# Index keys first, index products spread over four jobs, and attention taken two groups at a time with GpSimd scaling the probabilities

## The chip, the cores and the metric

The kernel runs on one core of one Trainium2 chip. The metric is device time in microseconds (us), the median of a few executions. The engines are named as the profile names them: PE is TensorE's matrix products (PEld its weight loads), DVE is VectorE, ACT is ScalarE, POOL is GpSimd, and SP is the queue that loads the weights.

## What is computed

One batch element of 512 tokens, 1024 wide, passes through three blocks in fp32: a gated block with a convolution and an mLSTM, then a block with sparse attention (A), then one with banded window attention (B), each with cross attention to 256 memory rows and a feed-forward stage. The change touches only how A and B attend. In A an indexer of 16 heads of 64 chooses which keys a query may see:

```python
dots = jnp.einsum('bqhd,bsd->bqhs', q_idx, k_idx)          # 16 heads of 64
score = jnp.einsum('bqhs,bqh->bqs', jax.nn.relu(dots), w_idx)
score = jnp.where(causal, score, -inf)
_, idx = lax.top_k(score, 128)                             # TOPK of 512 keys
s = (q_lat @ c_sel + q_rope @ kr_sel) * 128 ** -0.5        # 8 heads
o_lat = jax.nn.softmax(s) @ c_sel
```

B has 16 query heads of 64 over 4 key heads; a query sees the 128 keys up to itself, and one learned logit per head (a sink) joins the softmax's maximum and sum. The cross attention has 4 heads of 64 over 256 keys, with no mask.

## The kernel before, in words

All activations are held transposed, as 8 tiles of 128 features by 512 tokens. A dense product is done in **jobs**: 256 output columns of a weight matrix, 2 x 8 x 3 = 48 products of 128x128x512, three for each pair because operands are split into an upper and a lower fp32r half (L900). For each job SP loads the weights into one of two slots (the job's number decides which), ACT writes the upper half (L1581), POOL subtracts it for the lower half (`lower_job`, L2783), PE multiplies into a pair of banks, and DVE or ACT empties them. The order of the jobs is the table `STAGES`: in A four jobs `a_idx` (index queries, two tiles each), then `a_keys` (index key, rope part of the keys, index weights), `a_kv`, `a_qmem`, four `a_q`, `a_uk`, `a_uv`, and then attention and the output jobs `a_out`. Every engine has its own program, written out by hand; semaphores join them.

**The indexer.** The index queries and the index key are rotated before use. ACT copies the raw rows out, sends them by DMA to their partner rows (`partner_rows`), and DVE multiplies and adds (`turned`, L2567 and L2569), which counts in `rope_ready`. All of tiles 9 to 16 and the key tile 17 were rotated before the first index product. `dots` (L1418) then takes, for the query blocks b = 1, 2, 3 in turn and eight tiles each, two products of 64 rows (two heads), which are the 24 pairs of dots. ACT applies relu in the bank (L2068), and DVE multiplies by the head's weight and adds into `chosen` (L2710). Four pairs are put between the products of `a_kv` and 20 between those of `a_qmem` (at `DOTS_AFTER`). Blocks b = 1 end first here. When a block's sixteen heads are in, DVE runs 16 rounds of the eight largest (L2741) and their replacement (L2743), for b = 1, 2 and 3: 48 rounds of width 256, 384 and 512, with the rotation of the attention's queries (`turn_queries`) put between them at `ROPES_AT`. After the last round comes the mask (L2745), and behind it in DVE's program stands the first step of attention.

**Attention** (`attend`) runs over groups, one head or pair of heads by one block of 128 queries: 32 groups in A with keys 128, 256, 384 and 512 wide, 32 in B (two heads of 128 keys at b = 0, and of 256 at b = 1 to 3), and 8 for the memory behind each. 80 groups in all; a *unit* is four groups, b = 0 to 3. For a group, PE makes the scores (L1313: 128-row products in A, two side by side of 64 rows in B and memory), DVE adds the mask, scales and finds the row's extreme (L2612), ACT takes the exponential and its sum (L2003), DVE inverts the sum (L2628) and scales the probabilities (L2635), PE transposes them (L1322), ACT copies them out of the bank (L2012), and PE multiplies with the values (L1335; 64 columns each in B and memory). Per unit ACT copies the output (L2017) and DVE subtracts for its lower half (L2643). In B DVE first copies the sink into the columns beside the scores (L2607) and takes the lesser of extreme and sink (`lowest`, L2622). PE's program at step g is: scores of g, transposes of g - 3 (`LAG`), sums of g - 5 (`SUM_LAG`). Four of the products of the output job are put between the last steps (`FILL_AT`).

## Time and profile before

| | us |
|---|---|
| median of 3 runs | 2098.12 |
| lowest and highest | 2096.47, 2103.21 |
| the profiled execution | 2096.36 |
| its span, first to last instruction | 2094.6 |
| PE busy in the span | 2059.3 |

A product is counted busy until its modelled end, and each overlaps the next, so a busy PE may still be slower than it could be; what PE costs is read from the distance between the starts of products. The profile's waits show when an engine stood still and which instruction of which engine released it. The granted clock of PE is given as a share of 2.4 GHz.

### The profile page before, as it was taken

How to read it: one execution, taken by the hardware profiler on the slowest of the kernel's cores; microseconds unless marked ns; L12 is line 12 of the kernel's file. 1: busy time of each engine (PE TensorE's matmuls, PEld its weight loads, DVE VectorE, ACT ScalarE, POOL GpSimd, SP SyncE). 2: the span in 40 equal slices, each digit the busy share in tenths (PEclk: the TensorE clock that was granted, in tenths of full speed). 3: DMA queues.
4: the chain of work that ended last, by engine and by line, in shares of the span. 5: the costliest groups of instructions: out<-in, count | busy, mean ns of one | idle time of the engine just before them, and what ended most of it. 6: DMA issues, size and time to landing. Idle time of an engine off the chain costs nothing.

```text
span 2094.6 us, 28597 instructions
## 1 busy us (share of the span) xinstructions
PE 2059.3 (98%) x10618; PEld 1733.8 (83%) x10618; DVE 986.8 (47%) x1909; ACT 886.8 (42%) x1307; POOL 844.6 (40%) x281
## 2 busy tenths in 40 slices
PE   9999999999999999998999999999999999999998
PEld 6888877888888888884878888888887688888887
DVE  4889688573411111366985344134323934431432
ACT  3355445363443222534366454233423954432332
POOL 3443432444244444442712444444443034444443
PEclk9999999999999999999999999999999999999999
DMA  9654312325233342341202432433422034324322
GB/s 370 243 184 125 101 61 61 94 93 181 72 104 86 104 116 78 111 117 43 79 13 57 120 100 86 115 101 95 145 86 73 2 96 119 101 79 122 100 73 88
DMA packets 303799, 219.63 MB, mean 105 GB/s; under 512 B 13568, under 2 KB 288128, under 8 KB 301408
## 3 DMA queue, kind: packets, MB, share of 16 engines
q1 hardware_dynamic: 293216, 195.67, 31.1%
q10 hardware_dynamic: 10496, 22.81, 3.5%
q8 instruction: 53, 0.87, 0.2%
q14 instruction: 34, 0.28, 0.0%
HBM read 213.48 MB, written 2.10 MB: 103 GB/s over the span
## 4 chain that ended last, share of the span: by engine, by line
PE 64%; issue 18%; DVE 10%; POOL 5%; ACT 3%; ACTq 0%; POOLq 0%; DMA 0%; DVEq 0%
PE bank L900 51%; POOL w_split L2783 5%; PE bank L1123 2%; PE bank L1313 2%; PE bank L1335 2%; DVE bank L2280 2%; DVE arena L2743 1%; DVE small L2741 1%; DVE bank L2243 1%; PE bank L1322 1%; PE bank L1171 1%; DVE bank L2222 1%; POOL w_split_out L2783 1%; PE bank L1418 1%; PE bank L1271 1%
## 5 line engine op out<-in xcount | busy, mean ns | idle before, releaser
L900 PE MATMUL bank<-h_hi,w_split 128*128 128x512 f32 x3696 | 1119.3, 381 | 0.7 <-POOL w_split L2783 0.7
L2783 POOL TENSOR_TENSOR w_split<-wslots,w_split 128x2048 fp32r<-128x2048 f32 (+3 forms) x174 | 712.7, 4096 | 971.1 <-ACT w_split L1581 530.5
L900 PEld LDWEIGHTS bank<-h_hi,w_split 128*128 128x128 f32 x3696 | 698.0, 189 | 116.6 <-issue 17.5
L900 PE MATMUL bank<-h_lo,w_split 128*128 128x512 f32 x1848 | 701.3, 379 | 0.0
L900 PEld LDWEIGHTS bank<-h_lo,w_split 128*128 128x128 f32 x1848 | 349.3, 189 | 52.7 <-issue 5.2
L900 PE MATMUL bank<-hid_hi,w_split 128*128 128x512 f32 x1056 | 315.8, 379 | 1.9 <-DVE hid_lo L2525 1.9
L1602 ACT ACTIVATE w_split<-wslots 128x2048 fp32r<-128x2048 f32 (+2 forms) x80 | 141.3, 1767 | 367.9 <-PE bank L900 367.9
L1581 ACT ACTIVATE w_split<-wslots 128x2048 fp32r<-128x2048 f32 (+3 forms) x91 | 158.7, 1744 | 312.8 <-PE bank L900 287.1
L900 PEld LDWEIGHTS bank<-hid_hi,w_split 128*128 128x128 f32 x1056 | 199.6, 189 | 31.5 <-DVE hid_lo L2525 3.2
L900 PE MATMUL bank<-hid_lo,w_split 128*128 128x512 f32 x528 | 200.1, 379 | 0.0
L2243 DVE SCALAR_TENSOR_TENSOR bank<-arena,cols,bank 128x512 f32<-128x512 f32 x240 | 161.4, 749 | 5.5 <-ACT bank L1695 4.9
L2523 DVE TENSOR_TENSOR bank<-arena,bank 128x512 f32<-128x512 f32 x66 | 45.9, 696 | 210.6 <-ACT arena L1915 210.6
L2783 POOL TENSOR_TENSOR w_split_out<-wslots,w_split_out 128x320 fp32r<-128x320 f32 (+1 forms) x28 | 48.8, 1760 | 188.0 <-ACT w_split_out L1581 188.0
L900 PEld LDWEIGHTS bank<-hid_lo,w_split 128*128 128x128 f32 x528 | 99.8, 189 | 14.0
L2670 DVE TENSOR_TENSOR bank<-bank,rstd 128x512 f32<-128x512 f32 x44 | 30.8, 699 | 139.7 <-PE bank L900 139.3
L2482 DVE TENSOR_TENSOR xT<-xT,bank 128x512 f32 (+1 forms) x24 | 16.5, 688 | 139.8 <-PE bank L900 139.8
L2003 ACT ACTIVATE arena<-arena,small 128x257 f32<-128x257 f32 (+5 forms) x128 | 64.2, 503 | 30.3 <-DVE small L2612 16.9
L2525 DVE TENSOR_TENSOR hid_lo<-bank,hid_hi 128x512 f32 x66 | 45.6, 691 | 57.1 <-ACT hid_hi L1917 57.1
L1917 ACT ACTIVATE hid_hi<-bank 128x512 f32 (+1 forms) x66 | 39.4, 598 | 55.5 <-DVE bank L2523 55.5
L1313 PE MATMUL bank<-arena 64*128 64x256 f32 (+5 forms) x256 | 56.3, 425 | 6.2 <-DVE small L2612 4.7
L2675 DVE SCALAR_TENSOR_TENSOR arena<-bank,cols,arena 128x511 f32<-128x511 f32 x44 | 33.0, 750 | 58.1 <-ACT arena L1911 58.1
L563 DVE TENSOR_TENSOR bank<-bank,xT 128x512 f32<-128x512 f32 x24 | 16.9, 706 | 84.7 <-PE bank L900 84.7
(342 smaller groups left out, 2353.3 us busy)
## 6 DMA issues: line engine op xcount, KB each, us to landing
wslots<-in_f_w_up SPq DMA_DIRECT2D x88, 512.0 KB, 4.8
wslots<-in_w_in SPq DMA_DIRECT2D x24, 1024.0 KB, 5.4
wslots<-in_w_ffn_up SPq DMA_DIRECT2D x44, 512.0 KB, 4.6
arena<-in_w_ada ACTq DMA_DIRECT2D x8, 2048.0 KB, 8.9
wslots<-in_f_w_down SPq DMA_DIRECT2D x16, 768.0 KB, 4.8
wslots<-in_a_w_in SPq DMA_DIRECT2D x10, 1024.0 KB, 5.2
wslots<-in_f_w_down SPq DMA_DIRECT2D x16, 640.0 KB, 4.5
arena<-in_w_ada_first SPq DMA_DIRECT2D x8, 1024.0 KB, 18.9
```

What stands on the lines that cost most here:

```text
L900: return nc.tensor.matmul(bank[:], w, woven(x), start=start, stop=stop)
L1123: last = nc.tensor.matmul(banks[2 * p + b // 2][:, (b % 2) * 2 * P:(b % 2 + 1) * 2 * P], h_split[hp][:, c, b * P:(b + 1) * P], woven(w[wp] ...
L1313: last = nc.tensor.matmul(score_bank(g0 + g, e)[:, 0:n], q, kk, start=True, stop=True)
L1335: last = nc.tensor.matmul(unit_bank(unit)[lo:lo + n, b * P:(b + 1) * P], v, probs_turned[:, (g0 + g) % 3, at:at + P], start=(i == 0), stop ...
L1581: nc.scalar.activation(split_of(JOB_STAGE[n], p)[:, 0, 0:size], slot(p, 1, size)[:, 0, :], ACT.Copy).then_inc(hi_ready[p], 1)
L1602: nc.scalar.activation(split_of(name, p)[:, 0, 0:size], slot(p, 1, size)[:, 0, :], ACT.Copy).then_inc(hi_ready[p], 1)
L2003: last = nc.scalar.activation(part, part, ACT.Exp, bias=stat(n, 2 * with_sink + e), scale=-1.0, accum_out=stat(n, 4 + e))
L2243: ins = nc.vector.scalar_tensor_tensor(out=acc, in0=a_pad[:, c, k:k + T], scalar=dw_w[:, c, k:k + 1], in1=acc, op0=ALU.mult, op1=ALU.add)
L2280: ins = nc.vector.scalar_tensor_tensor(out=acc, in0=woven(qk[:, t, k:k + T]), scalar=qk_w[:, t, k:k + 1], in1=acc, op0=ALU.mult, op1=ALU.add)
L2523: nc.vector.tensor_tensor(halves(banks[2 * p][:]), halves(up_gate[:, p, :]), plain(banks[2 * p + 1][:]), ALU.mult).then_inc(S["hid_made"], 1)
L2525: nc.vector.tensor_tensor(hid[1][:, 0:tiles, :][:, t, :], banks[2 * p][:], hid[0][:, 0:tiles, :][:, t, :].bitcast(F32), ALU.subtract).then ...
L2783: last = nc.gpsimd.tensor_tensor(part[:, 1, cols_of], slot(p, 1, size)[:, 0, cols_of], part[:, 0, cols_of].bitcast(F32), ALU.subtract)
```

## The change

**Order of jobs.** `a_keys` comes before the four `a_idx`, so the key tile is rotated first. Each index query tile is rotated after its job, and its dots follow. The 24 pairs go, two tiles at a time and over b = 1, 2, 3, five between the products of each of `a_idx` 2 and 3, eight in `a_kv` (the last six in twos) and six in `a_qmem` (in twos, at products 6, 14 and 22). The first 12 pairs have only banks 5 and 6, so each waits until DVE has used the pair before it. In DVE's program relu's results are weighted (`weighted`) between the rotations. The norm of the latent (`latent_norm`) and the emptying of `a_qmem` move into the rounds of b = 1. PE waits for the former before `a_q`. The rotations of the attention's queries move to later rounds.

**Attention.** PE takes two groups at a step: scores of 2i and 2i + 1, transposes of 2i - 3 and 2i - 2, sums of 2i - 5 and 2i - 4. POOL scales the probabilities in place of DVE, in a new `attend` of its own, with the four pieces of the output job's lower half between groups 30 to 33. ACT copies the transposes of even groups, DVE those of odd ones. In B the sink is given to L2612 as the starting value of its minimum, so `lowest` goes. The eight copies of the key's rope rows, done by POOL before, are one DMA from ACT's queue.

```diff
-    ... ("a_idx", 4), ("a_keys", 1), ("a_kv", 1), ("a_qmem", 1), ...
+    ... ("a_keys", 1), ("a_idx", 4), ("a_kv", 1), ("a_qmem", 1), ...
-        ROPES_AT = {(2, 2): (0, 2), (3, 0): (2, 4), (3, 3): (4, 6), (3, 7): (6, 8)}
+        ROPES_AT = {(2, 8): (0, 2), (3, 2): (2, 4), (3, 9): (4, 6), (3, 13): (6, 8)}
+        DOTS = [(t, b) for j in range(3) for b in range(1, TB) for t in (2 * j, 2 * j + 1)] + [(t, b) for b in range(1, TB) for t in (6, 7)]
+        DOTS_AT = {("a_idx", 2): [(i, k, k + 1) for k, i in enumerate((10, 18, 27, 38, 46))],
+                   ("a_idx", 3): [(i, k + 5, k + 6) for k, i in enumerate((10, 18, 27, 38, 46))],
+                   ("a_kv", 0): [(8, 10, 11), (17, 11, 12), (30, 12, 14), (38, 14, 16), (46, 16, 18)],
+                   ("a_qmem", 0): [(6, 18, 20), (14, 20, 22), (22, 22, 24)]}
+        LATE_DOTS = 12
+        dot_bank = lambda n: banks[(5, 6)[n % 2] if n < 2 * LATE_DOTS else (4, 7, 5, 6)[n % 4]]
...
# PE, attend
-                for g in range(len(groups) + SUM_LAG):
-                    if g < len(groups):
-                        scores(g)
...
-                    if LAG <= g < len(groups) + LAG:
-                        turn(g - LAG)
-                    if g >= SUM_LAG:
-                        sums(g - SUM_LAG)
+                steps = len(groups) // 2
+                for i in range(steps + 3):
+                    of_groups(scores, 2 * i)
...
+                    of_groups(turn, 2 * i - 3)
...
+                    of_groups(sums, 2 * i - 5)
# PE, the dots
+            def dots(first, end):
+                for k in range(first, end):
+                    t, b = DOTS[k]
+                    pe.wait_ge(S["rope_ready"], 10 if k >= LATE_DOTS else 2 + t + 1)
+                    for e in range(2):
+                        before = dot_before(2 * k + e)
+                        if before is not None:
+                            pe.wait_ge(S["relu_used"], before + 1)
...
+            pe.wait_ge(S["norm_ready"], TILES_BEFORE["kv"] + 2)
             for j in range(4):
                 split_job(start_split("a_q", j), DT, 2 * P, h_parts, None)
# DVE, attend
-                def weights(g):
-                    n = g0 + g
-                    steps.settle()
-                    for e, (lo, w) in enumerate(groups[g]["heads"]):
-                        part = probs[:, n % RING, lo:lo + w]
-                        last = nc.vector.tensor_scalar(part, part, stat(n, e), None, ALU.mult)
-                    last.then_inc(S["at_probs"], 1)
+                def copies(g):
...
+                    nc.vector.tensor_copy(probs_turned[:, n % 3, 0:w], banks[6 + n % 2][:, 0:w]).then_inc(S["odd_copied"], 1)
...
+                    if g % 2 and 5 <= g < len(groups) + 4:
+                        copies(g - 4)
# POOL
+            def attend(k, output):
+                g0, groups = GROUPS_BEFORE[k], ATTENTION[k] + ATTENTION[k + 1]
+                for g, grp in enumerate(groups):
+                    n = g0 + g
+                    pool.wait_ge(S["at_inverse"], n + 1)
+                    for e, (lo, w) in enumerate(grp["heads"]):
+                        part = probs[:, n % RING, lo:lo + w]
+                        last = nc.gpsimd.tensor_scalar(part, part, stat(n, e), None, ALU.mult)
+                    last.then_inc(S["at_probs"], 1)
+                    if 30 <= g < 34:
+                        lower_piece(output, ahead(output), g - 30)
```

PE in the middle of B's attention. L1313 (L1323 in the changed kernel) are scores, L1322 (L1332) transposes and L1335 (L1345) sums; before, one unit and the next group stand so in a row:

```order
L1313 MATMUL bank<-arena 128x256 x2
L1322 MATMUL bank<-cons,arena 128x128 x4
L1335 MATMUL bank<-arena 64x128 x4
L1313 MATMUL bank<-arena 128x256 x2
L1322 MATMUL bank<-cons,arena 128x128 x4
L1335 MATMUL bank<-arena 64x128 x4
```

and now, for two steps of two groups:

```order
L1323 MATMUL bank<-arena 128x256 x4
L1332 MATMUL bank<-cons,arena 128x128 x6
L1345 MATMUL bank<-arena 64x128 x8
L1323 MATMUL bank<-arena 128x128 x2
L1323 MATMUL bank<-arena 128x256 x2
L1332 MATMUL bank<-cons,arena 128x128 x8
L1345 MATMUL bank<-arena 64x128 x6
```

The same products stand in half as many runs of one kind. POOL, at the place between the last rotation of A's queries and the first piece of `a_out`'s weights, before:

```order
L2927 TENSOR_TENSOR arena<-arena 32x512 x2
L2949 COPY arena<-arena 32x512 x8
L2783 TENSOR_TENSOR w_split_out_63<-wslots,w_split_out_63 128x320 x4
L2783 TENSOR_TENSOR w_split_out_64<-wslots,w_split_out_64 128x320 x4
```

and now, the first five of 48 scalings (32 groups of one head, 8 of two) behind the rotation:

```order
L2965 TENSOR_TENSOR arena<-arena 32x512 x2
L3003 ISA
L3003 TENSOR_SCALAR arena<-arena,small 128x128
L3003 TENSOR_SCALAR arena<-arena,small 128x256
L3003 TENSOR_SCALAR arena<-arena,small 128x384
L3003 TENSOR_SCALAR arena<-arena,small 128x512
```

The copies are gone from POOL and the scalings have come. PE in `a_qmem`, where L900 (L910) are the job's own products and L1418 (L1431) pairs of dots, before, at b = 2 (the pattern of the 20 pairs):

```order
L1418 MATMUL bank<-arena 128x384 x2
L900 MATMUL bank<-h_lo,w_split_52 128x512
L900 MATMUL bank<-h_hi,w_split_52 128x512
L1418 MATMUL bank<-arena 128x384 x2
L900 MATMUL bank<-h_hi,w_split_52 128x512
L900 MATMUL bank<-h_lo,w_split_52 128x512
L1418 MATMUL bank<-arena 128x384 x2
```

and now, for the two pairs of tiles 6 and 7 at b = 2, with the products before and behind them:

```order
L1431 MATMUL bank<-arena 128x256 x4
L910 MATMUL bank<-h_lo,w_split_52 128x512
L910 MATMUL bank<-h_hi,w_split_52 128x512 x2
L910 MATMUL bank<-h_lo,w_split_52 128x512
L910 MATMUL bank<-h_hi,w_split_52 128x512 x2
L910 MATMUL bank<-h_lo,w_split_52 128x512
L910 MATMUL bank<-h_hi,w_split_52 128x512
L1431 MATMUL bank<-arena 128x384 x4
```

The 24 pairs stand at 18 places instead of 24, and the last of them behind the 22nd product of `a_qmem` instead of the 44th. DVE, around the first round of the eight largest (L2741, `MAX`; L2776 in the changed kernel), before. L2710 (L2626) is the weighting, L2722 (L2655) the latent's norm, L2560 (L2570) the emptying of `a_qmem`:

```order
365 L2710 SCALAR_TENSOR_TENSOR arena<-bank,small,arena 128x512 x3
366 L2722 SCALAR_TENSOR_TENSOR arena<-arena,cols,bank 128x512 x2
367 L2710 SCALAR_TENSOR_TENSOR arena<-bank,small,arena 128x512 x12
368 L2560 TENSOR_TENSOR arena<-bank,rstd 128x512 x2
369 L2725 TENSOR_SCALAR bank<-trig,cons 32x512
370 L2741 MAX small<-arena 128x8
371 L2743 MATCH_REPLACE arena<-small,arena 128x256
```

and now:

```order
374 L2626 SCALAR_TENSOR_TENSOR arena<-bank,small,arena 128x512 x4
375 L2649 RECIPROCAL square<-square 128x128
376 L2776 MAX small<-arena 128x8
377 L2778 MATCH_REPLACE arena<-small,arena 128x256
...
384 L2655 SCALAR_TENSOR_TENSOR arena<-arena,cols,bank 128x512 x2
385 L2776 MAX small<-arena 128x8
...
391 L2570 TENSOR_TENSOR arena<-bank,rstd 128x512 x2
392 L2660 TENSOR_SCALAR bank<-trig,cons 32x512
393 L2776 MAX small<-arena 128x8
```

The norm and the emptying went from ahead of the first round to behind the fourth and the seventh.

## Rows read from the trace of the kernel before

**Rows 1.** The page's part 1: engine, busy us, share of the span, instructions.

```profile
PE 2059.3 (98%) x10618; PEld 1733.8 (83%) x10618; DVE 986.8 (47%) x1909; ACT 886.8 (42%) x1307; POOL 844.6 (40%) x281
```

**Rows 2.** PE's waits, whole run: who for whom, total us, times, longest.

```profile
PE bank L1313 <- DVE small L2612: 4.7, 1, 4.7
PE bank L1418 <- DVE arena L2710: 3.3, 3, 1.8
...
PE bank L1418 <- DVE arena L2569: 2.2, 1, 2.2
PE bank L1322 <- ACT arena L2012: 2.0, 4, 0.7
```

**Rows 3.** PE's timeline, A's attention starts: start, duration, instruction, [idle before].

```profile
1058.37 0.82 PE L1313 MATMUL bank<-arena 128*128 128x128 f32 x4
1063.85 3.36 PE L1313 MATMUL bank<-arena 128*128 128x384 f32 x4 [4.66 <-DVE small L2612]
```

**Rows 4.** Windows: length; PE, PEld, DVE, ACT, POOL busy; clock, DMA, GB/s.

```profile
1061.40:1068.10 6.70, 4.25 (x10) 2.38 (x10) 4.87 (x19) 1.82 (x7) 0.00 (x0) 0.50 0.00 0
1629.54:1636.18 6.64, 6.64 (x60) 4.12 (x58) 6.30 (x40) 6.25 (x22) 0.00 (x0) 1.00 0.00 1
```

**Rows 5.** Timeline of DVE, from the last weighting to the last round.

```profile
995.84 1.29 DVE L2560 TENSOR_TENSOR arena<-bank,rstd 128x512 f32<-128x512 f32 x2
...
997.89 0.43 DVE L2741 MAX8 small<-arena 128x8 f32<-128x256 f32 x1
...
1063.03 0.43 DVE L2745 TENSOR_SCALAR arena<-arena 128x512 f32<-128x512 f32 x1
```

**Rows 6.** Timeline of PE in `a_qmem`: a pair of dots between products.

```profile
968.36 0.70 PE L900 MATMUL bank<-h_hi,w_split 128*128 128x512 f32 x2
968.99 0.92 PE L1418 MATMUL bank<-arena 64*128 64x384 f32 x4
969.84 0.48 PE L900 MATMUL bank<-h_lo,w_split 128*128 128x512 f32 x1
```

**Rows 7.** Waits of DVE from 899 to 998 us.

```profile
DVE bank L2567 <- DMA arena<-arena: 13.8, 4, 5.6
```

**Rows 8.** Timeline of PE in B's attention, one group.

```profile
1632.78 0.70 PE L1313 MATMUL bank<-arena 64*128 64x256 f32 x4
1633.41 0.66 PE L1322 MATMUL bank<-cons,arena 128*128 128x128 f32 x4
1633.99 0.66 PE L1335 MATMUL bank<-arena 128*64 128x128 f32 x8
```

**Rows 9.** Timeline of PE near its end: two groups' sums together.

```profile
1685.23 1.15 PE L1335 MATMUL bank<-arena 128*64 128x128 f32 x16
1686.30 0.48 PE L900 MATMUL bank<-b_out_hi,w_split_out 128*128 128x512 f32 x1
```

**Rows 10.** Timeline of PE in A's attention, where all tiles are whole.

```profile
1086.80 0.60 PE L1322 MATMUL bank<-cons,arena 128*128 128x128 f32 x4
1087.24 0.61 PE L1335 MATMUL bank<-arena 128*128 128x128 f32 x4
```

**Rows 11.** Timeline of POOL, 990 to 1060 us.

```profile
995.89 0.46 POOL L2907 TENSOR_TENSOR arena<-arena,cons 128x128 f32<-128x128 f32 x1 [14.27 <-DVE arena L2710]
...
1002.53 2.52 POOL L2913 TENSOR_TENSOR kv_lo<-arena,kv_hi 128x512 fp32r<-128x512 f32 x2
...
1053.15 4.49 POOL L2949 COPY arena<-arena 32x512 f32<-32x512 f32 x8
```

**Rows 12.** Lines by form, 1622.9 to 1671 us: count, busy us, mean ns.

```profile
L2635 DVE TENSOR_SCALAR arena<-arena,small 128x256 f32<-128x256 f32 x44 | 14.9, 381 | 0.1
...
L2012 ACT ACTIVATE arena<-bank 128x512 f32<-128x512 f32 x21 | 12.1, 575 | 0.0
```

**Rows 13.** Timeline of DVE as POOL begins a piece at 1662.42.

```profile
1661.36 0.16 DVE L2622 TENSOR_TENSOR small<-small,cols 128x2 f32<-128x2 f32 x1
...
1663.44 0.68 DVE L2622 TENSOR_TENSOR small<-small,cols 128x2 f32<-128x2 f32 x1
```

364 lines of the change are left out of this document (191 added, 173 removed).

## The prediction

> **What bounds the kernel now.** I read the page's first part, then the waits of PE, then PE's timeline where the change acts. PE is busy for 2059.3 of 2094.6 us [rows 1] with 10618 products, a count the change doesn't touch. So time can come only from three things: waits of PE; what is lost when the shape of its tiles changes; and its clock. The waits near the change are few: 4.66 us at the start of A's attention for L2612, which stands in DVE's program behind the last round, 3.3 and 2.2 of dots, and 2.0 of transposes at four places [rows 2, 3]. The clock: from 1061.4 to 1068.1 PE's granted clock reads 0.50, the lower level of 1.2 GHz, which came after PE had stood still for 2 us [rows 4], and the first products behind the wait are slow: four, mostly of 384 columns, take 3.36 us [rows 3].
>
> The third thing is hidden in "busy". The reader is to see it in a group of B [rows 8]: scores, transposes and sums start 0.63 and 0.58 us apart, and the sums take another 0.60 to the next group's scores. In A, where every tile is 128x128, four transposes take 1087.24 - 1086.80 = 0.44 [rows 10], so the same four cost 0.14 more in B, between scores of 64 rows and sums of 64 columns. Sixteen sums in a row start 1.07 before what follows [rows 9], and twice eight take 2 x 0.60: 0.12 lost by the break. Two scores of 256 columns on half the rows each are four products; at the rate of transposes (0.11 per 128 columns, halves side by side), they stream in 4 x 0.107 = 0.43, and they take 0.63: 0.20 lost. So one group of B or memory loses about 0.46 to changes of shape, and one of A none.
>
> **Fewer changes of shape.** Two groups at a step halve the number of changes: each pair saves at most 0.20 + 0.14 + 0.12 = 0.46. There are 16 pairs in B and 4 + 4 of memory, so 24 x 0.46 = 11. If the 0.20 in the scores belonged to the products and not to the change, it is 24 x 0.26 = 6.2. A's 16 pairs give nothing, since their tiles are all whole. I take all 0.46, by the same argument that gave the other two numbers, and then see whether the others keep up, since PE's unit of four groups would fall from 6.64 to about 6.64 - 2 x 0.46 = 5.7.
>
> **The other engines at that pace.** In one unit of B, DVE is busy 6.30 and ACT 6.25 of 6.64 [rows 4]; they are as full as PE. DVE loses seven scalings at 0.28 to 0.38 (44 of 256 columns take 0.381 each [rows 12]), 2.5, and `lowest` at 0.16 twice or so, 0.3 to 0.5 [rows 13]; it gains two copies of four and of fewer tiles, as ACT now has them, 0.575 [rows 12], 1.15. DVE stands at 4.7 to 5.0. ACT loses those copies, 6.25 - 1.1 = 5.15. Both are below 5.7. POOL gets seven scalings. No row shows its price: POOL copies 32x512 at 4.49 / 8 = 0.56 each with one input, and multiplies two inputs in 0.46 for 128 columns and 2.52 / 2 = 1.26 for 512 [rows 11], which is 0.73 at 256. The scaling has one tensor as input, so the copy is nearest: a start of about 0.2 (0.46 less 128 columns of the slope) and 0.36 / 2 for half its width, 0.4; I take 0.45, and keep 0.28 (half the copy, with no start) and 0.73 as ends. Then 7 x 0.45 = 3.2 of 5.7: POOL has room for pace.
>
> Latency is tighter. A step lasts 2.8, and the transposes of group 2i - 2 follow its scores by one step and a half, about 3.9 us from the scores' start. In between come the scores 0.70 [rows 8], L2612 at 0.42 twice, the exponential at 0.5 twice and its sums at 0.2 twice, and the inverse at 0.16 (all in the same timelines), and POOL's two scalings 0.9, with some hand-overs: 3.6 to 4.3. Some steps will wait a little. Before, the distance was three groups, 5.5 us. I take three quarters of the 11 us: **8.3**. Ends: 2 (every step waits 0.4) and 11.
>
> DVE and POOL disturb each other: as POOL began a piece, the L2622 beside it took 0.68 instead of 0.16 [rows 13]. Those of two inputs are gone from DVE's attention after the change but for one in four groups (the lower half of the output), so I price this at nothing; 14 scalings longer by 0.3 would still be below PE's pace.
>
> The Trainium skill has a rule against this change: GPSIMD Engine Reference, 3.1, holds that elementwise work goes to DVE, with a two-input add of 2048 taking twice as long on GpSimd. By its factor on DVE's 0.38 a scaling is an estimated 0.76, which is the upper end of my bound, and no row has a one-input multiply on POOL to judge it; the sum above goes by the copy's row. The time by it is the first rival's. The same skill, SBUF — State Buffer, Who interferes with whom, says that DVE with two SBUF inputs locks against GpSimd's reads; by that rule, the trace agrees (0.68 against 0.16).
>
> **Start of A's attention.** DVE's rounds run from 997.89 to 1063.46, 65.6 us, without rest [rows 5]; PE has begun the first four scores at 1058.37, and waits from 1059.19 to 1063.85 [rows 3]. The first round had to wait for the last of `dots`, behind product 44 of 48 of `a_qmem` and begun at 992.43 in PE's timeline, whose weighting ends at 995.84, and for the emptying of that job and a table, 2.05 more [rows 5]. Now the last dots stand behind product 22. Removed from ahead: 22 products at 0.216, 4.8; and those 2.05 and the latent's norm (two instructions, 1.3) now lie inside the rounds, 3.3. Added ahead: the dots of tiles 0 to 5 no longer wait for all the rotations, but each pair of the first 12 waits for DVE, as only two banks serve it. DVE had 13.8 us of waits for the partner rows' DMA [rows 7] in this stretch and has work to fill them now; PE has a gap of 8 to 10 products (about 2 us) between pairs, and a pair's relu and weighting take some 1.6: tight but enough. The key tile first and each index tile behind its own job leave the DMA (5.6 at most [rows 7]) one job of 10.5 us. I let PE be 0 to 5 late in all on these, and take 1 more of waits than before (3.3 + 2.2).
>
> So the last weighting ends at about 995.8 - 4.8 - 2.5 (below) + 1 = 989.5, the rounds start about 990 and last 65.6 + 3.3 = 68.9: 1058.9 instead of 1063.46. PE's arrival: the 24 pairs were at 24 places, and are at 18. A place costs two changes: four products of 384 columns stream in 2 x 0.32 and take 969.84 - 968.99 = 0.85, 0.21 lost, and two products before it take 0.63 instead of 0.43 [rows 6], 0.20. Six fewer: 6 x 0.41 = 2.5 earlier. New waits of PE behind the dots: `a_q` waits for the norm, which DVE reaches four rounds (3.7 us) after the first: about 990 + 3.7 + 1.5 = 995.2, against PE's end of `a_qmem` at about 994.8 - 2.5 + 1 = 993.3. I take 2. PE comes to the attention at 1058.4 - 2.5 + 1 + 2 = 1058.9. The 4.66 go nearly whole (0.2 to 0.8 stays for the first L2612): I take **4.7**, ends 1 and 7. What is late next is either side, as both arrive within 1 us.
>
> With the wait goes the lower clock. From 1063.85 to 1068.1, 4.25 us, PE works at half rate, and half of that is lost [rows 3, 4]: 2.1, and some of it hides behind DVE's first groups: **2.0**. If a wait of some 2 us stays, so may this: 0 to 2.2. The copies of the key's rope rows leave POOL, where they ended at 1057.64 [rows 11], before anyone needed them: nothing. The queues moved past: POOL's lower half of the first `a_idx` stands behind other work, 0.3 later.
>
> **Start of B's attention.** Some of the 2.0 of waits for L2012 [rows 2] fall there, and the copies are shared now: 1, ends 0 and 1.4.
>
> **Sum.** 8.3 + 4.7 + 2.0 + 1.0 - 0.3 = 15.7. The profiled execution is 2096.36, 1.76 over its span of 2094.6 and 1.8 under the median 2098.12: 2080.7 by its own time, and **2081** with some of that difference.
>
> **The rivals.** (1) *POOL is slow*: at 0.73 a group's two scalings take 1.5 on a path that has 3.9 for 3.6 to 4.3, each step of B waits 0.6, and attention gives 3: 2086. For it: POOL's only multiplies are at that price [rows 11]. Against: those read two tensors. (2) *The rounds don't start earlier*: the two-bank dots wait for DVE, DVE for the partner rows, and PE loses over 5 us in `a_idx`, `a_kv`: the start gives 1 and the clock stays: 2086. For: rows 7 show that a rotation can hang 5.6 us on its DMA, and DVE's program now has the weighting behind it. Against: a whole job lies between. Both together: 2092. (3) *All ideal*: 11 + 7 + 2.2 + 1.4: 2075, 2071 if A gains as well. (4) *Slower: POOL sets the pace.* A unit of the memory has eight scalings of 256, of B seven; A's, of 128 to 512 columns, are on average as long as one of 320. PE's units are 5.7 and 5.5, so POOL decides from about 0.75 each, and at 1.3 (its start of 0.2 and two-input slope doubled) the units are 9.1 to 10.4: some 12 of B and memory lose 4 each, 48, and A some 8 x 0 to 3, less the gain: 2120 and more. The point where it cancels the whole gain is about 1.0. No row is above 0.73 at this width. (5) *It doesn't do what it says*: scores 2i and 2i + 1 need two banks free, and if PE waits between them, the shape changes stay beside waits: within 2 us of now, 2096.
>
> **How the numbers follow.** Main case .44, rival 1 .18, rival 2 .15, both .07, ideal .07, slower .06, no effect .03. The range takes the main case with its ends (2075 to 2086), rivals 1 and 2 whole, half of ideal and most of both: 2072 to 2092 holds .83. A difference below 0.3%, 6.3 us, can't be told from none: faster ends at 2091.8. Main, 1, 2 and 3 are faster (.84); of "both" half is: .03 more, but some of 1 and 2 isn't, so .85; same .09 (the other half, no effect, and those); slower .06.
>
> **What would show it.** In B, transposes and sums stand in runs of eight and 16, and a unit of four groups takes 5.7 to 6.0 in PE's timeline; waits of L1332 for POOL's scaling would be rival 1. POOL's group 128x256 reads 0.33 to 0.5. The first round starts near 990, A's first wait for L2612's successor is under 1 us, and the clock stays at 1.00 there. PE's waits for dots (L1431) sum to at most 7, and its wait ahead of `a_q` to about 2. I am wrong if POOL's scalings end as late as PE's transposes begin, if the two-bank dots wait at each place, or if A's steps change, which I priced at zero.

## The result, and the profile after

The changed kernel took 2110.65 us, the median of 8 runs (2106.62 to 2112.21), and the kernel before 2101.24, the median of 8 (2096.47 to 2103.21). The ratio is 1.0041, with a 95% interval of 1.0032 to 1.0051: **slower by some 9 us**, where 2081 and faster was forecast. The profiled execution took 2109.66 with a span of 2107.9. One execution each of `pcopy` (6008.19 us), `mix` (4108.83), `split` (2155.58) and the kernel before (3072.52), in the experiments below, ran in a slow state and is left out of every ratio.

The page's first part (engine, busy us, share of the span, instructions), to be held against [rows 1]:

```profile
PE 2056.2 (98%) x10618; PEld 1739.2 (83%) x10618; DVE 972.1 (46%) x1789; ACT 869.1 (41%) x1267; POOL 956.0 (45%) x401
```

PE is busy 3 us less and stands still 16 us more. The waits of PE over the whole run say for whom, to be held against [rows 2]:

```profile
PE bank L1332 <- POOL arena L3003: 16.3, 24, 2.0
PE bank L1323 <- DVE small L2681: 4.2, 8, 2.3
...
PE bank L1431 <- DVE arena L2626: 0.9, 2, 0.5
```

L1332 are the transposes and L3003 is the scaling on POOL: 16.3 us, 24 times. The waits for the dots fell from 5.5 us to 0.9, and that for L2681 (L2612 before) at the start of A's attention from 4.66 to 2.25. The profiled executions, cut at the same products of PE (us):

| stretch of PE's program | before | after | difference |
|---|---|---|---|
| up to the first product of A's index jobs | 887.32 | 889.97 | +2.65 |
| index jobs to the first scores of A | 171.05 | 171.86 | +0.81 |
| A's attention and its memory | 69.43 | 72.08 | +2.65 |
| from there to B's first scores | 482.41 | 482.45 | +0.04 |
| B's attention and its memory | 76.09 | 83.37 | +7.28 |
| the rest of the span | 408.27 | 408.13 | -0.14 |

The first line has nothing to do with the change. In the fourteen profiles here, of kernels that share all the work up to there, it reads from 887.3 to 890.2, and the profiled execution of before has the lowest. What is left is +10.6 us, nearly all of it in the two attentions. B's 7.28 fall in two parts: up to the first scores of the memory 3.5, and the memory's eight groups 3.8.

What a scaling costs, from the lines by form of POOL:

```profile
L3003 POOL TENSOR_SCALAR arena<-arena,small 128x256 f32<-128x256 f32 x88 | 79.8, 922 | 15.0 <-DVE small L2689 14.9
L3003 POOL TENSOR_SCALAR arena<-arena,small 128x128 f32<-128x128 f32 x24 | 14.3, 603 | 14.3 <-DVE small L2689 14.3
L3003 POOL TENSOR_SCALAR arena<-arena,small 128x512 f32<-128x512 f32 x8 | 12.5, 1564 | 0.0
L3003 POOL TENSOR_SCALAR arena<-arena,small 128x384 f32<-128x384 f32 x8 | 9.9, 1242 | 3.6 <-DVE small L2689 3.5
```

The four sizes lie on a line, 0.28 us + 2.5 ns a column: 0.922 at 256 columns, where 0.45 was taken and 0.73 was the upper bound. One unit of B in PE's timeline, 7.40 us from the scores at 1639.80 to those at 1647.19; before it took 6.64 to 6.65 [rows 4]:

```profile
1639.80 1.13 PE L1323 MATMUL bank<-arena 64*128 64x256 f32 x8
1640.86 0.93 PE L1332 MATMUL bank<-cons,arena 128*128 128x128 f32 x6
1641.72 1.14 PE L1345 MATMUL bank<-arena 128*64 128x128 f32 x16
1642.80 0.49 PE L1323 MATMUL bank<-arena 64*128 64x128 f32 x4
1643.54 0.70 PE L1323 MATMUL bank<-arena 64*128 64x256 f32 x4 [0.25 <-DVE small L2681]
1644.30 0.63 PE L1332 MATMUL bank<-cons,arena 128*128 128x128 f32 x4
1645.79 0.66 PE L1332 MATMUL bank<-cons,arena 128*128 128x128 f32 x4 [0.87 <-POOL arena L3003]
```

The longer runs do what was meant: eight scores of 256 columns take 1.06 where twice four took 1.26, and sixteen sums take 1.08 where twice eight took 1.20. But the eight transposes are cut in two by a wait for POOL. The chain of work that ended last says what the unit is made of (start, us, what):

```profile
1639.77 0.60 ACT arena L2019
1640.36 0.49 ACT b_out_hi L2024
1640.85 0.98 ACT arena L2010 x4
1641.84 0.02 issue
1641.86 0.17 DVE small L2689
1642.03 0.08 issue
1642.12 3.63 POOL arena L3003 x4
1645.75 0.04 issue
1645.79 0.66 PE bank L1332 x4
1646.45 0.63 PE bank L1345 x8
```

It is a loop, and the same pieces come again 7.40 us later: four scalings in a row, the two groups b = 1 and 2, 3.63 us; the transposes of b = 2; the sums; ACT's copy (L2019), which waits for them, and its copy of the output (L2024); the exponentials (L2010) queued behind these; the inverse (L2689); and POOL again at +7.40. POOL's price stands in it four times, and the rest is 3.77.

In A a step reads so:

```profile
1072.67 0.82 PE L1323 MATMUL bank<-arena 128*128 128x128 f32 x4
1073.33 0.38 PE L1332 MATMUL bank<-cons,arena 128*128 128x128 f32 x2
1073.92 0.55 PE L1332 MATMUL bank<-cons,arena 128*128 128x128 f32 x3 [0.21 <-POOL arena L3003]
1074.31 1.28 PE L1345 MATMUL bank<-arena 128*128 128x128 f32 x10
```

The wait is put down at 0.21, but five transposes take 1074.31 - 1073.33 = 0.98 where the row behind it in the next step has 0.54: here the wait costs 0.44, half of it not shown as idle. A's unit went from 5.49 (before) to 5.92, and eight of them make 3.4 us. In the memory's groups POOL also has the four pieces of the output weight between its scalings:

```profile
1675.64 0.86 POOL L2990 TENSOR_TENSOR w_split_out<-wslots,w_split_out 128x320 fp32r<-128x320 f32 x1
1676.48 1.82 POOL L3003 TENSOR_SCALAR arena<-arena,small 128x256 f32<-128x256 f32 x2
1678.27 0.86 POOL L2990 TENSOR_TENSOR w_split_out<-wslots,w_split_out 128x320 fp32r<-128x320 f32 x1
```

From 1673.85 to 1689.79 it is never idle, and two groups take 5.26 us, against some 3 of PE's work. So in the memory POOL's own pace is the bound: the chain of releases, followed back through this stretch, stays on POOL from 1673.85 to 1686.20. PE's longest wait for a scaling is there, and the granted clock reads 0.68 from 1680 to 1684:

```profile
1680.99 0.72 PE L1332 MATMUL bank<-cons,arena 128*128 128x128 f32 x4 [1.97 <-POOL arena L3003]
1681.64 2.03 PE L1345 MATMUL bank<-arena 128*64 128x128 f32 x16
```

Sixteen sums take 2.03 where they take 1.14 elsewhere, so this costs more than the wait itself.

The index part: the first round starts at 992.39, 102.42 us behind the first index product, where before it was 110.57 [rows 5]. That is 8.15 earlier. Yet the rounds' end came only 1.6 earlier. Of the 6.6 between, 3.3 are the norm and the emptying, which now stand inside the rounds. The rest is the mask of b = 1 (L2780). The timeline of DVE, and under it POOL's:

```profile
1011.12 3.89 DVE L2780 TENSOR_SCALAR arena<-arena 128x256 f32<-128x256 f32 x1
```

```profile
1010.31 4.55 POOL L2818 TENSOR_TENSOR w_split<-wslots,w_split 128x2048 fp32r<-128x2048 f32 x1 [4.27 <-ACT w_split L1591]
```

The mask of b = 1 took 0.39 before. Now it began 0.8 us into a piece of POOL's and ended 0.15 behind it: 3.5 us lost.

### The profile page after: what moved, and what is told of

Its sections match the earlier page's. It is cut to its first block, busy times and chain, and to the rows that moved or that the text cites. A ratio compares the mean times of both kernels' runs of the same rounds, so it can differ in the third digit from the quotient of the medians.

```text
span 2107.9 us, 28567 instructions
## 1 busy us (share of the span) xinstructions
PE 2056.2 (98%) x10618; PEld 1739.2 (83%) x10618; DVE 972.1 (46%) x1789; ACT 869.1 (41%) x1267; POOL 956.0 (45%) x401
## 4 chain that ended last, share of the span: by engine, by line
PE 77%; DVE 9%; POOL 5%; ACT 3%; issue 3%; DMA 1%; SPq 0%; ACTq 0%; DVEq 0%; POOLq 0%
PE bank L910 67%; POOL arena L3003 3%; PE bank L1133 2%; DVE bank L2290 2%; DVE arena L2778 1%; PE bank L1281 1%; DMA wslots<-in_w_glu 1%; DVE small L2776 1%; DVE bank L2253 1%; PE bank L1431 1%; PE bank L1181 1%; PE bank L1345 1%; DVE bank L2232 1%; PE bank L1332 1%; ACT w_split L1591 1%
## 5 line engine op out<-in xcount | busy, mean ns | idle before, releaser
L910 PE MATMUL bank<-h_hi,w_split 128*128 128x512 f32 x3696 | 1118.0, 381 | 3.2 <-POOL w_split L2873 1.4
L910 PEld LDWEIGHTS bank<-h_hi,w_split 128*128 128x128 f32 x3696 | 697.9, 189 | 117.7 <-issue 17.5
L910 PE MATMUL bank<-h_lo,w_split 128*128 128x512 f32 x1848 | 701.1, 379 | 0.0
L910 PEld LDWEIGHTS bank<-h_lo,w_split 128*128 128x128 f32 x1848 | 349.3, 189 | 51.2 <-issue 3.4
L910 PE MATMUL bank<-hid_hi,w_split 128*128 128x512 f32 x1056 | 315.9, 379 | 1.9 <-DVE hid_lo L2535 1.9
L910 PEld LDWEIGHTS bank<-hid_hi,w_split 128*128 128x128 f32 x1056 | 199.6, 189 | 31.4 <-DVE hid_lo L2535 3.2
L910 PE MATMUL bank<-hid_lo,w_split 128*128 128x512 f32 x528 | 200.1, 379 | 0.0
L3003 POOL TENSOR_SCALAR arena<-arena,small 128x256 f32<-128x256 f32 (+3 forms) x128 | 116.0, 922 | 32.9 <-DVE small L2689 32.7
L910 PEld LDWEIGHTS bank<-hid_lo,w_split 128*128 128x128 f32 x528 | 99.8, 189 | 14.1
L2010 ACT ACTIVATE arena<-arena,small 128x257 f32<-128x257 f32 (+5 forms) x128 | 64.0, 504 | 21.6 <-DVE small L2681 20.7
L1332 PE MATMUL bank<-cons,arena 128*128 128x128 f32 x256 | 41.7, 283 | 18.4 <-POOL arena L3003 16.3
L1332 PEld LDWEIGHTS bank<-cons,arena 128*128 128x128 f32 x256 | 27.9, 140 | 38.5 <-POOL arena L3003 28.4
```

The lines of the kernel that those rows point to most:

```text
L910: return nc.tensor.matmul(bank[:], w, woven(x), start=start, stop=stop)
L1332: last = nc.tensor.transpose(banks[6 + (g0 + g) % 2][:, j * P:(j + 1) * P], probs[:, (g0 + g) % RING, at:at + P], con("ident"))
L2010: last = nc.scalar.activation(part, part, ACT.Exp, bias=stat(n, e), scale=-1.0, accum_out=stat(n, 4 + e))
L3003: last = nc.gpsimd.tensor_scalar(part, part, stat(n, e), None, ALU.mult)
```

## The experiments

Each run is given with its median and with its ratio (95% interval) to the kernel before, run beside it on the same chip. A and B are the us from the first scores to the first product behind the last sums in the profile, and the unit is B's in the steady part.

| run | us | ratio | A | B | unit |
|---|---|---|---|---|---|
| kernel before | 2100.7 to 2103.6 | 1 | 69.4 | 76.1 | 6.65 |
| changed kernel | 2110.65 | 1.0041 (1.0032 to 1.0051) | 72.1 | 83.4 | 7.40 |
| dve_all | 2097.83 | 0.9980 (0.9969 to 0.9992) | 66.7 | 76.9 | 6.83 |
| dve_single | 2096.78 | 0.9974 (0.9961 to 0.9987) | 65.5 | 77.1 | 6.61 |
| half | 2091.14 | 0.9948 (0.9931 to 0.9965) | 65.3 | 72.9 | 6.49 |
| pcopy | 2087.12 (one execution) | none | 63.7 | 70.4 | 6.48 |
| mask | 2108.78 | 1.0038 (1.0027 to 1.0049) | 72.0 | 83.4 | 7.40 |
| masks2 | 2107.62 | 1.0027 (1.0013 to 1.0041) | 71.2 | 85.3 | 7.40 |
| pool_single | 2110.20 | 1.0033 (1.0021 to 1.0046) | 73.4 | 84.2 | 7.37 |
| mix | 2101.80 | 0.9997 (0.9986 to 1.0007) | 64.8 | 84.2 | 7.41 |
| single_masks | 2093.40 | 0.9959 (0.9945 to 0.9973) | 63.3 | 75.7 | 6.61 |
| split | 2090.80 | 0.9944 (0.9927 to 0.9961) | 62.4 | 74.4 | 6.80 |
| sinks | 2094.30 | 0.9964 (0.9951 to 0.9977) | 63.0 | 76.5 | 6.86 |
| sinks_split | 2093.34 | 0.9955 (0.9943 to 0.9966) | 62.7 | 76.7 | 6.99 |

**All scaling back on DVE.** Theory: POOL's scaling is what PE waits for. Rival: the step of two groups leaves too little distance, whatever engine scales.

```diff
 # POOL, attend (excerpt)
-                    last = nc.gpsimd.tensor_scalar(part, part, stat(n, e), None, ALU.mult)
 # DVE, behind inverses(g - 1)
+                    last = nc.vector.tensor_scalar(part, part, stat(n, e), None, ALU.mult)
 # ACT copies odd groups too
 ...
```

> The changed kernel with every scaling back on DVE (behind the inverse of its group) and every copy of the transposes back on ACT; PE's steps of two groups stay. Theory 1, GpSimd's scaling is what PE waits for: the 16.3 us of PE's waits on it go, A's unit falls from 5.92 to the 5.49 us of before, B's unit from 7.40 to about 6.3 (ACT is busy for 6.25 of it), and the time is 15 us under the changed kernel, about 2095. Theory 2, the step of two groups leaves too little distance between a group's scores and its transposes whatever engine scales: PE waits for DVE instead, B's unit stays above 6.8, and the time stays above 2103.

2097.83, 13 us under the changed kernel: the theory holds for the loss. But the unit of B came to 6.83 and not 6.3, longer than before, and A's to 5.71 and not 5.49. PE waits now for ACT's copies (7.2 us, 19 times) and for L2681, so the rival is right in part. (The run also moves the copies of the odd groups to ACT; `half` and pcopy below change POOL's instruction alone.)

**And one group at a step.**

```diff
-                    of_groups(scores, 2 * i)
...
-                    of_groups(turn, 2 * i - 3)
...
-                    of_groups(sums, 2 * i - 5)
+                        scores(g)
...
+                        turn(g - 3)
...
+                        sums(g - 5)
```

> As dve_all, and PE takes one group at a step as before; with it only the index part of the change (and the sink as a starting value) is left. If two groups at a step are worth what the changes of shape suggest (0.46 us a pair, 24 pairs), this is up to 8 us over dve_all, B's unit about 6.5; if ACT's 6.25 us in a unit of B bound both, the two are within 2 us. Against the kernel before: the index part takes 0.8 us more up to the start of A's attention and gives back 2.4 us of wait and 2 of low clock, so 2 to 4 us faster, about 2098.

2096.78, no difference to dve_all: with DVE scaling, steps of two groups are worth nothing, since what PE saves in changes of shape it waits for ACT and DVE. Against the kernel before it is 0.26% faster, and the profile puts the gain at the start of A's attention, so to the index part: A's 65.5 is 3.9 under 69.4. B's attention is 1.0 longer than before. Its first three units are 1.7 longer, and the clock reads 0.92 there after PE's first waits, which is 1.6 of 20.4 us by itself:

```profile
1609.60:1630.00 20.40, 18.83 (x129) 11.14 (x130) 17.45 (x88) 14.71 (x53) 0.00 (x0) 0.92 0.00 2
```

In the steady part the unit is 6.61 against 6.65, although four `lowest` of 0.16 to 0.18 us are gone. The lines by form of DVE between 1629 and 1669 us show why, before and in dve_single:

```profile
L2612 DVE CUSTOM_DVE_ANT_0 arena<-bank,cons 128x256 f32<-128x256 f32 x36 | 13.7, 418 | 0.0
```

```profile
L2690 DVE CUSTOM_DVE_ANT_0 arena<-bank,cons,cols 128x256 f32<-128x256 f32 x32 | 14.1, 479 | 0.0
```

With its starting value read from a column, the instruction takes 0.061 us more, eight times a unit, 0.5, which is most of what the four had cost. In the memory of the same run, where there is no sink and no column, it is back at 0.419.

**The dose: POOL scales half the columns.** The output's other half is left unscaled.

```diff
-                        last = nc.gpsimd.tensor_scalar(part, part, stat(n, e), None, ALU.mult)
+                        last = nc.gpsimd.tensor_scalar(part[:, 0:w // 2], part[:, 0:w // 2], stat(n, e), None, ALU.mult)
```

> The changed kernel with GpSimd scaling only the first half of each head's columns (the other half is left unscaled); nothing else differs. By the four sizes in the trace a scaling takes 0.28 us + 2.5 ns a column, so 0.60 instead of 0.92 at 256 columns. Theory 1: B's unit falls from 7.40 to about 5.9, A's from 5.92 to 5.5, most of the 16.3 us of waits go and the time is 12 to 15 us under the changed kernel, about 2097. Theory 2: GpSimd's price hardly counts, 3 us or less.

2091.14, 19.5 us less for 0.32 us less per scaling of 256. More than either theory had: A's unit is back at 5.49, and B's fell to 6.49. The loop explains the latter: at 0.604 it needs 3.77 + 4 x 0.6 = 6.2, so another bound holds at 6.49 (more on it under pcopy).

**The copy's price.** The scaling is replaced by a copy in place.

```diff
-                        last = nc.gpsimd.tensor_scalar(part, part, stat(n, e), None, ALU.mult)
+                        last = nc.gpsimd.tensor_copy(part, part)
```

> GpSimd copies each head's probabilities in place (TENSOR_COPY with one input) instead of scaling them; the scaling is left out. The prediction priced the scaling by the copy of 32x512 at 0.56 us, 0.4 to 0.45 at 256 columns. If one input is what makes the copy cheap, this copy takes about 0.4 here, the scaling's 0.92 comes from the multiply, and the time is that of the run `half` or a little less, 2090. If 128 rows instead of 32 are what makes it dear, the copy takes about 0.9 too and the time stays at 2110.

The lines by form of POOL:

```profile
L3003 POOL COPY arena<-arena 128x256 f32<-128x256 f32 x88 | 33.1, 403 | 48.6 <-DVE small L2689 48.6
...
L3003 POOL COPY arena<-arena 128x512 f32<-128x512 f32 x8 | 4.9, 616 | 3.3 <-DVE small L2689 3.2
```

0.403 at 256 columns, which is what the prediction had for the scaling. So the copy's row was read rightly and was the wrong row: a copy costs 0.83 ns a column and this multiply 2.5, more even than the two-input rows of [rows 11] (2.1). The kernel took 2087.12 in its one execution, 16 us under the median of before beside it (2102.87): with the price that was assumed the change would have been faster, but still 6 short of 2081. B's unit stays at 6.48, not 5.7. Windows 1630 to 1660 of this run (length; PE, PEld, DVE, ACT, POOL busy; clock, DMA share, GB/s):

```profile
1630.00:1660.00 30.00, 27.14 (x262) 19.55 (x264) 27.07 (x126) 24.88 (x87) 13.83 (x38) 1.00 0.01 2
```

DVE is busy for 27.07 / 30 x 6.48 = 5.85 a unit, where 4.7 to 5.0 was predicted, and PE waits for L2681. The chain in this profile closes a loop of 6.47 us: PE's scores, transposes and sums 0.70, 1.07 and 0.63; ACT's copy, output and exponentials 0.60, 0.49 and 0.98; DVE's lower half of the output (L2704) 0.67, sink 0.24 and L2681 0.40; and hand-overs.

This run also has what the changes of shape are worth when nothing interrupts PE. Its eight transposes in a row:

```profile
1638.09 1.07 PE L1332 MATMUL bank<-cons,arena 128*128 128x128 f32 x8
1639.09 0.88 PE L1345 MATMUL bank<-arena 128*64 128x128 f32 x12
```

They take 1.00, where two times four took 2 x 0.58 = 1.16 [rows 8].

**The mask.** Does POOL's piece make L2780 long, and does it hold A's start?

```diff
                     steps.did(nc.vector.match_replace(left, small[:, 96:104], left, CHOSEN))
+                    if (b, k) == (2, 5):
+                        masked(1)
...
```

> The changed kernel with the mask of b = 1 (L2780, 3.89 us there where it took 0.39 before, while GpSimd ran the 4.55 us piece of a weight's lower half) moved behind the fifth round of b = 2, where GpSimd is idle. If the lock with GpSimd made it long, it takes 0.4, the rounds end 3.5 us earlier, and PE's first waits of A's attention (2.25 + 0.46) go: 2 to 3 us faster than the changed kernel, 2108. If the instruction is long for another reason, it is 3.9 at the new place too and nothing changes.

The expected gain of 2 to 3 us didn't show: the intervals of this run and of the changed kernel overlap. The mask of b = 1 took 0.29 away from POOL's piece, which speaks for the piece as what had made it long. But then the mask of b = 2 came earlier and met the next piece. DVE's and POOL's timelines:

```profile
1033.46 3.23 DVE L2768 TENSOR_SCALAR arena<-arena 128x384 f32<-128x384 f32 x1
```

```profile
1031.91 4.55 POOL L2825 TENSOR_TENSOR w_split<-wslots,w_split 128x2048 fp32r<-128x2048 f32 x1 [0.88 <-ACT w_split L1591]
```

It started 1.55 us into the piece and ended 0.23 behind it. (The place is behind the sixth round of b = 2, not the fifth.) Both masks were then moved, that of b = 2 behind the second round of b = 3:

```diff
+                    if (b, k) in ((2, 5), (3, 1)):
+                        masked(b - 1)
```

> The run `mask` took 0.29 us for the mask of b = 1, but the rounds of b = 3 then began 3.5 us earlier and the mask of b = 2 fell on GpSimd's next piece (3.23 us instead of 0.36). Here the changed kernel has the mask of b = 1 behind the sixth round of b = 2 and that of b = 2 behind the second round of b = 3, both where GpSimd is idle. Lock as the cause: both take 0.3 to 0.4, the rounds end 3 us earlier, PE's wait of 2.25 us at the start of A's attention goes, and the time is 2 to 2.5 us under the changed kernel (2108). Otherwise nothing.

Both took 0.29 and 0.36, and PE's wait at the start of A's attention went from 2.25 to none (A's waits for L2681: 0.5 in all). A's attention gained 0.9 and the arrival at it came 1.1 later in its profile (172.9 us behind the first index product, for 171.9); the median is 3.0 under the changed kernel, but the intervals of the two overlap, so this pair alone doesn't settle the size. A loss stands in the same profile, at the start of B:

```profile
1614.20:1630.00 15.80, 14.04 (x86) 9.47 (x86) 10.50 (x53) 9.19 (x35) 11.27 (x14) 0.78 0.00 1
```

The clock of PE reads 0.78 there, and B took 85.3. It is the lower clock of 1.2 GHz, as in [rows 4], in a stretch where PE had waited; where it falls differs from run to run. The other pair is dve_single with the same edit:

> dve_single (DVE scales, ACT copies, one group at a step, so only the index part and the sink as a starting value of the change) with the two masks moved as in masks2. The index part with its lock taken away: PE's wait of 2.3 us at the start of A's attention goes, 2 to 2.5 us under dve_single, about 2094.5 (0.996 of the kernel before). If the rounds' end wasn't what held A's start, equal to dve_single.

2093.40 against 2096.78, and A's attention 63.3 against 65.5, with waits of 0.6 us in place of 2.8. The intervals of the two ratios overlap here too, and another 1.4 of the difference lie in B, where dve_single's profile has its stretch of low clock and this one has none. So what is shown for the masks is 2.2 us in A's attention; the size in the whole time isn't.

**Is it POOL's pace or its lateness?** POOL scales, and PE takes one group at a step.

> The changed kernel with PE taking one group at a step (scores of g, transposes of g - 3, sums of g - 5); GpSimd still scales. If GpSimd's pace is what counts (6.58 us busy in B's unit and eight times 0.92 = 7.4 in the memory's), B's attention stays at 82 to 84 us; A's unit, where GpSimd is busy for 4.3 of 5.92 us and only its lateness counts, goes back to 5.5, and the total is some 4 us under the changed kernel. If the short distance is what counts in B too, B's unit goes to 6.8 and the total is 8 us or more under it.

2110.20, the same as the changed kernel. B's unit is 7.37, POOL being busy for 6.76 of it:

```profile
1639.83 6.76 POOL L3000 TENSOR_SCALAR arena<-arena,small 128x256 f32<-128x256 f32 x8 [0.60 <-DVE small L2686]
1647.19 6.76 POOL L3000 TENSOR_SCALAR arena<-arena,small 128x256 f32<-128x256 f32 x8 [0.60 <-DVE small L2686]
```

So the grouping neither causes nor cures the loss. A's unit didn't go back to 5.5 as expected; it rose to 6.24, with waits for the scheme's other piece, DVE's copies of the odd transposes (L2694: 3.4 us in A's attention, 8.0 in the whole run), which stand in DVE's program where the step of two wants them.

**POOL relieved of a quarter.** With both masks moved as in masks2, DVE scales A and the groups b = 0 of B and memory, and ACT copies three groups in four; POOL has 5.5 us in B's unit.

```diff
+        on_pool = lambda n, e: n >= 32 and n % 4 > 0
+        act_copies = lambda n: n % 4 != 1
```

> masks2, and the scalings divided: DVE scales in A and in the groups of b = 0 of B and memory, GpSimd in the other three; ACT copies the transposes of three groups in four and DVE those of b = 1. GpSimd is then busy for 5.5 us in a unit of B, DVE for about 5.7 and ACT for 5.9. By the price of GpSimd as the cause: no waits in A's steps (unit 5.49), B's unit about 6.1, B's attention 73 to 75 us, and the total 17 to 20 us under the changed kernel, about 2092. If three engines at 5.5 to 5.9 of 5.65 wait for each other through the lock or through PE's order, B's unit is 6.5 or more and the total no better than dve_all, 2096.

2101.80, where some 2092 was expected. A's attention fell to 64.8, and B's unit stayed at 7.41, within a hundredth of that of masks2 and of the changed kernel, though POOL had less to do. This fells the reading that POOL's pace is the bound in B's units. POOL in that run:

```profile
1640.55 5.46 POOL L3036 TENSOR_SCALAR arena<-arena,small 128x256 f32<-128x256 f32 x6 [1.95 <-DVE small L2701]
1647.97 5.46 POOL L3036 TENSOR_SCALAR arena<-arena,small 128x256 f32<-128x256 f32 x6 [1.95 <-DVE small L2701]
```

It is idle for 1.95 us each unit. The chain in the same run has the same loop: POOL's four of b = 1 and 2 for 3.64, transposes 0.67, sums 0.63, ACT 0.60 + 0.49, exponentials and inverse. What was taken off POOL (b = 0) isn't in the loop.

**Each group divided.** With the masks moved, POOL scales the second head of B and memory, DVE the first and all of A, so one scaling in place of two lies on that loop per group.

```diff
+        on_pool = lambda n, e: n >= 32 and e == 1
```

> The masks moved, steps of two groups, and each group of B and memory divided: GpSimd scales its second head, DVE its first; A is scaled by DVE; ACT copies three of four. GpSimd is busy for 3.4 us in B's unit and one scaling (0.92) instead of two in a row (1.84) lies between the inverse and the transposes. In the run `mix` GpSimd was idle for 2 us of a unit of 7.5, so the row of waits through GpSimd, PE, DVE and ACT bound it and not its pace. If that row is the cause, PE's waits for GpSimd go and DVE, busy for some 6.5 us, sets the unit: B at 75 to 77, total 2093 to 2096. If it is GpSimd beside DVE as such (the lock), B stays above 80.

2090.80, a ratio of 0.9944: the lowest median of a kernel with the whole computation, below the kernel before and the changed one. PE's waits for POOL's scaling are 0.5 us in the whole run. B's unit is 6.80, the waits being for DVE (busy for 27.35 of 30 us), and the gain over single_masks (2.6 us) isn't shown, as the intervals overlap. B's steady units are longer than before (6.80 against 6.65), and the whole of B is 1.7 shorter, so what it gains lies in the groups around them. A step in it for which the profile shows no wait has:

```profile
1646.77 1.28 PE L1342 MATMUL bank<-cons,arena 128*128 128x128 f32 x8
1647.98 0.88 PE L1355 MATMUL bank<-arena 128*64 128x128 f32 x12
```

Eight transposes take 1.21, no less than two times 0.58 [rows 8]. But they aren't one run: the third and fourth transposes start 0.11 behind the one before them, and the fifth, the first of the second group, 0.24. In pcopy there is no such break, and eight take 1.00. What makes the break isn't shown; the second group's own wait stands at that place.

**Sinks by POOL.** The masks are moved, the two sink columns of a group are written by POOL, and all scaling is on DVE; in a second version POOL also scales the second head of b = 2 and 3.

```diff
-                        nc.vector.tensor_copy(columns, ...)
+                    nc.gpsimd.tensor_copy(columns, ...)   # POOL, behind at_scores
```

> The masks moved, steps of two groups, all scaling on DVE; GpSimd only writes the two sink columns of each group of B (a copy of 128x2, DVE's before) and ACT copies the transposes in B and memory. DVE is relieved of 0.16 us four times a unit and is then busy for about 5.7, ACT for about 6.0, so a unit of B takes 6.1 to 6.3 us and B's attention 74: total about 2091. If DVE and ACT wait for each other as in dve_all (76.9 us), the gain stays under 1 us a stage and the total is 2094.

> As the run `sinks`, and GpSimd also scales the second head of b = 2 and 3 in B and memory (1.84 us a unit, never two in a row), and DVE copies the transposes of b = 1 in place of ACT. DVE about 5.6, ACT 5.4, GpSimd 2.4 us busy in a unit whose products take 5.65: B's unit 5.9, total about 2088. If a scaling of 0.92 on the path makes the transposes wait all the same, no better than `sinks`.

2094.30 and 2093.34, where 2091 and 2088 were expected: units of 6.86 and 6.99, no better than `split` or single_masks. Relieving DVE of four small copies didn't shorten B's unit.

## Why the prediction was wrong, point by point

- **POOL's price: the step that failed.** "The scaling has one tensor as input, so the copy is nearest": 0.45 was taken, and it is 0.922. pcopy shows that the copy's price was right for a copy (0.403), and with 0.604 in `half` and 0.403 in pcopy the loss becomes a gain of 0.5% and, in one execution, of 0.75%. The upper end of 0.73 was no bound: it stood on the two-input rows (0.46 at 128 columns, 1.26 at 512), and the scaling costs more than these at each size, 0.603 and 1.564. The GPSIMD Engine Reference of the Trainium skill, 3.1, speaks for DVE with a factor of 2, and the trace has 0.922 against 0.381 [rows 12], 2.4: by that rule the estimate of 0.76 was nearer than the prediction's 0.45. (The 0.381 holds some scalings that ran beside POOL's pieces; in B's steady units DVE takes 0.351, and the factor is 2.6.)
- **How POOL enters the unit: half right.** Rival 4 (slower) had POOL's pace as its mechanism and about 0.75 as the point from which it decides. In B that pace would be 6.7 a unit, and mix shows that it is not what bounds: the loop of two groups with four scalings is, 3.77 + 4p. By this sum, an estimate from the one chain, it passes 6.65 from p = 0.72, so the prediction's point "about 1.0", where the price cancels the whole gain, was too high: at 0.922 the change already loses. In the memory rival 4's pace is what bounds, with the weight's pieces on POOL besides, and that is 3.8 of B's 7.3 us. The first rival (a wait at each step of B, 0.6) is the form that came, at a higher price: 0.87 + 0.25 us of waits a unit and what they break.
- **A's 16 pairs "give nothing": wrong.** They lost 0.43 a unit, 3.4 us, for POOL's lateness, and this wasn't priced: in `half` and pcopy A's unit is back at 5.49. The memory's pieces of the weight, which stand between POOL's scalings, weren't priced either.
- **Fewer changes of shape: the terms were right, the gain wasn't collected.** Scores 0.20 and sums 0.12 a pair were measured, and for the transposes 0.16 in pcopy where 0.14 was taken. In the changed kernel a wait cuts the eight transposes in two, in `half` (1.19) and `split` (1.21) the break that no wait shows, and the term is lost. The three quarters of 11 us that the prediction took for them presumed that the other engines answer within PE's 5.7.
- **"DVE stands at 4.7 to 5.0" and PE's unit at 5.7: wrong.** In pcopy DVE is at 5.85 and the unit at 6.48. The sink as a starting value costs 0.06 eight times, a copy of transposes 0.67 twice where 0.575 was taken, and DVE's copy of the sink 0.25 four times beside POOL's work where it took 0.16 before; the last is a disturbance of the kind that the prediction priced at nothing. (It also counted seven scalings and two `lowest` a unit, where there are eight, two of them of 128 columns, and four; this would leave DVE less to do, not more.) The second fault is the method: that every engine's busy time is below 5.7 doesn't make the unit 5.7, since the loop from PE over ACT and DVE back to PE takes 6.47. The shape term can be collected only if ACT and DVE keep up, and dve_all against dve_single shows that nothing of it came.
- **The start of A's attention.** The first round was predicted at 990 and came at 992.39 in a run that was 2.65 late: right to 0.3. PE's arrival was predicted 0.5 us later and came 0.8 later. The clock stayed at 1.00 at this place: right, and of the 6.7 us taken for waits and clock together A's attention gained 3.9 in dve_single and 6.1 in single_masks. The changed kernel had a stretch of low clock elsewhere, in B's memory. The rounds lasted 72.1 where 68.9 was predicted and so ended 3.0 later, for the mask, and that cost 2.25 + 0.46 of waits. The prediction named the lock of DVE and POOL ("beside it took 0.68 instead of 0.16") and priced it "at nothing" for attention; it didn't ask which DVE instruction the earlier rounds would move onto POOL's pieces. The Trainium skill, SBUF — State Buffer, Who interferes with whom, lists `tensor_scalar` among the operations that can take the pair shared with GpSimd, and says that the loser fully blocks. By that rule, the trace agrees: 3.89 and 3.23 us where 0.29 to 0.39 is the price, ending with POOL's piece both times.
- **The start of B's attention** was to give 1.0: its first three units took 19.04 for 19.33, so 0.3.
- **Still open:** what holds B's unit at 6.48 to 6.5 in `half` and pcopy, against an estimated 5.7 of PE's pieces without waits (1.07 + 0.81 + 1.07 + 1.00 + 0.81 in pcopy, and about 0.95 for the scores of b = 0 and 1), is read from the chain (copies, outputs and exponentials in ACT's order, then DVE), and no run took it away. That POOL's work is what makes the sink's copy long is argued from 0.16 with POOL idle against 0.25. Nor was a run made with the memory's pieces elsewhere.

## What to carry to other kernels

Price an operation on an engine by a row of the same operation, and where there is none, say that the nearest row is no bound; then put the price into the loop that a value goes round, as often as it stands there, not only into the engine's sum of busy time. Here longer runs of one tile shape paid PE's price back only where no group had to wait, so ask of each engine in that loop whether it can still answer in the shorter time. And when work moves earlier, look at what it now stands beside: an instruction that was cheap at its old place may meet another engine's long one at the new, and the next one after it as well.

## What the runs showed of the hardware

- A `TENSOR_SCALAR` on GpSimd with a column as its scalar took 0.603, 0.922, 1.242 and 1.564 us for 128, 256, 384 and 512 columns; a `COPY` took 0.296, 0.403, 0.510 and 0.616.
- A DVE `TENSOR_SCALAR` of 128x256 that began inside a 4.55 us instruction of GpSimd took 3.89 instead of 0.29 to 0.39.
- A wait of 0.21 us among PE's transposes in A cost 0.44. Eight transposes of B took 1.00 in one run and 1.21 where the fifth started 0.24 instead of 0.11 behind the fourth, with no idle time shown.
- DVE's copy of two sink columns took 0.25 beside GpSimd's copies in pcopy and 0.16 in dve_single, where GpSimd stood still.
- Reading the starting value of DVE's multiply, add and minimum from a column added 0.061 us to 0.418 at 256 columns.
